# First adaptive chunks as one-column TensorE products between the first projections

## What is computed

```python
cond = jax.nn.silu(c)                                   # c: (1, 1024)
for i in range(DEPTH):                                  # 2 layers
    shift, scale, gate = jnp.split(cond @ ada_w[i] + ada_b[i], 3, axis=-1)   # ada_w[i]: (1024, 3072)
    h = rms_norm(x, norm_g[i]) * (1 + scale[:, None, :]) + shift[:, None, :]
    y = nsa_mixer(h, ...) if i % N_MIXERS == 0 else moba_mixer(h, ...)
    x = x + gate[:, None, :] * y
# in nsa_mixer
q, kc, vc, ks, vs, kw, vw, gl, z = split_cols(h @ w_in, [...])
# kc, vc go through a block compressor (gelu(flat @ cmp_w1 + b1) @ cmp_w2); ks, kw are normed and rotated
```

## Time and profile before

| | us |
|---|---|
| median of 3 runs | 1037.69 (1036.21 to 1040.94) |
| profiled execution, its own time | 1035.83 |
| its span, first to last instruction | 1034.0 |
| TensorE busy | 937.6 |
| VectorE busy | 604.4 |
| ScalarE busy | 522.7 |
| GpSimd busy | 189.5 |

### The profile page before, as it was taken

How to read it: one execution, slowest core, us unless ns; L and a number is a source line. 1 busy time by engine, 2 the same in 40 slices (tenths; PEclk the granted TensorE clock), 3 DMA queues, 4 the chain that set the end, 5 groups by cost and what they waited for, 6 DMA issues and landing times.

```text
span 1034.0 us, 13297 instructions
## 1 busy us (share of the span) xinstructions
PE 937.6 (91%) x4855; PEld 765.9 (74%) x4855; DVE 604.4 (58%) x1178; ACT 522.7 (51%) x956; POOL 189.5 (18%) x204
## 2 busy tenths in 40 slices
PE   0299998798989978989999998999899889999997
PEld 0288987455668955778888887888788778888886
DVE  5765447976457478555555544658345745555542
ACT  4243446775435477454444443667555444444431
POOL 4305504663002660000000000326000200000000
PEclk9999999987699999999999999999999999999999
DMA  8654735544055452435655653545233544555551
GB/s 314 239 188 140 235 126 172 163 147 139 0 163 166 141 183 82 156 108 176 207 168 183 203 169 113 194 143 167 81 101 111 169 146 165 183 191 196 187 160 41
DMA packets 45391, 163.28 MB, mean 158 GB/s; under 512 B 5136, under 2 KB 5392, under 8 KB 45328
## 3 DMA queue, kind: packets, MB, share of 16 engines
q1 hardware_dynamic: 45328, 162.44, 48.8%
HBM read 161.37 MB, written 1.05 MB: 157 GB/s over the span
## 4 chain that ended last, share of the span: by engine, by line
PE 80%; DVE 9%; issue 5%; ACT 4%; DMA 1%; POOL 1%; SPq 0%; POOLq 0%; DVEq 0%; ACTq 0%
PE bank L445 52%; PE bank L454 11%; PE bank L469 4%; PE bank L498 3%; PE bank L594 3%; PE bank L573 2%; PE bank L572 1%; DVE ada_acc L1367 1%; PE bank L531 1%; PE bank L596 1%; DVE soft L1460 1%; DVE stats L1449 1%; ACT soft L974 1%; PE bank L593 1%; DMA pos<-in_positions 1%
## 5 line engine op out<-in xcount | busy, mean ns | idle before, releaser
L855 ACT ACTIVATE w_hi<-w_raw 128x1024 fp32r<-128x1024 f32 (+2 forms) x249 | 259.5, 1047 | 210.7 <-PE bank L445 187.7
L1277 DVE TENSOR_TENSOR w_lo<-w_raw,w_hi 128x1024 fp32r<-128x1024 f32 (+2 forms) x249 | 300.8, 1224 | 111.0 <-ACT w_hi L855 110.9
L445 PE MATMUL bank<-w_hi,h_hi 128*128 128x512 f32 (+1 forms) x576 | 227.5, 395 | 2.7 <-DVE h_lo L1814 2.7
L445 PE MATMUL bank<-w_hi,h_lo 128*128 128x512 f32 (+1 forms) x576 | 224.2, 389 | 0.0
L445 PE MATMUL bank<-w_lo,h_hi 128*128 128x512 f32 (+1 forms) x576 | 223.8, 389 | 0.0
L445 PEld LDWEIGHTS bank<-w_hi,h_hi 128*128 128x128 f32 x576 | 108.6, 189 | 23.7 <-issue 3.0
L445 PEld LDWEIGHTS bank<-w_hi,h_lo 128*128 128x128 f32 x576 | 108.5, 188 | 22.5
L445 PEld LDWEIGHTS bank<-w_lo,h_hi 128*128 128x128 f32 x576 | 108.8, 189 | 20.8
L1895 POOL TENSOR_TENSOR ada_acc<-ada_acc,w_raw 128x512 f32<-128x512 f32 x70 | 93.1, 1330 | 87.4 <-ACT w_raw L859 80.7
L454 PE MATMUL bank<-h_hi,w_hi 128*128 128x256 f32 x264 | 77.9, 295 | 0.2 <-ACT tok_k L859 0.2
L454 PE MATMUL bank<-h_lo,w_hi 128*128 128x256 f32 x264 | 75.3, 285 | 0.0
(11 more groups left out here) (256 smaller groups left out, 1455.7 us busy)
## 6 DMA issues: line engine op xcount, KB each, us to landing
w_raw<-in_weights SPq DMA_DIRECT2D x298, 512.0 KB, 4.0
w_raw<-in_weights SPq DMA_DIRECT2D x4, 360.0 KB, 3.2
x<-in_x SPq DMA_DIRECT2D x1, 1024.0 KB, 10.2
gate_bias<-in_gate_bias SPq DMA_DIRECT2D x2, 512.0 KB, 9.1
out<-x SPq DMA_DIRECT2D x1, 1024.0 KB, 4.0
w_raw<-in_weights SPq DMA_DIRECT2D x3, 256.0 KB, 2.6
const<-in_constants SPq DMA_DIRECT2D x1, 413.5 KB, 3.1
cols<-in_columns SPq DMA_DIRECT2D x1, 208.5 KB, 3.9
```

The costliest lines, as they stand in the source:

```text
L445: mm = e.matmul(pb[t][:, 0:n], xs[q], ws[p], start=(k + kk == 0 and i == 0), stop=(k + kk == kts - 1 and i == 2))
L855: e.activation(w_hi[i % NSPLIT][:, 0:c], raw[v % NRAW][:, 0:c], ACT.Copy).then_inc(*rounded(v))
L1277: e.tensor_tensor(w_lo[i % NSPLIT][:, 0:c], raw[v % NRAW][:, 0:c], w_hi[i % NSPLIT][:, 0:c].bitcast(F32), ALU.subtract).then_inc(*rested(v))
```

## The change

- `ada_products` on TensorE takes over the first four chunks: the raw unit is the stationary operand, block by block, and `cond` the one moving column. The four results of a chunk stand in four columns of a bank, summed over the eight blocks there. ScalarE, GpSimd and VectorE no longer touch these units.
- The units are reordered: chunk 0 (shift) and chunk 2 (scale) of the first four feature blocks come first; then units of chunks 1 and 3 stand between the first two units of `nsa_kcvc` and of `nsa_kskw`, which need only those four blocks of h. TensorE's list follows that order. The pairing stands behind the third `nsa_kskw` unit, not the second.
- `norm_modulates` and `norm_rounds` run in two halves, two pairs each; a fourth bank (7) takes the fourth turned pair in the first layer.
- `rotation_tables` is split: the angles stay first on VectorE, the tables move behind the second half of `norm_modulates`. On ScalarE the squares of x stand ahead of sine and cosine.
- The first DMAs are columns, unit 0, x, constants, unit 1, positions, rows, then the other units.

```diff
-    order = (ada(0, 0, 4)
-             + one("nsa_kcvc") + one("nsa_kskw") + one("nsa_q0") + one("cmp_w1_0", CJ, 256, False)
+    early, kcvc, kskw = ada(0, 1, 2) + ada(0, 3, 4), one("nsa_kcvc"), one("nsa_kskw")
+    order = (ada(0, 0, 1) + ada(0, 2, 3)
+             + [kcvc[0]] + early[0:3] + [kcvc[1]] + early[3:6] + [kskw[0]] + early[6:8] + [kskw[1]]
+             + kcvc[2:] + kskw[2:] + one("nsa_q0") + one("cmp_w1_0", CJ, 256, False)
...
+            def ada_products(c, bank, free):
+
+                w.wait_ge(*cond_done.at())
+                w.wait_ge(*free)
+                for u in of[f"ada0_{c}"]:
+                    w.wait_ge(*fetched[u % NRAW].at(u))
+                    for kk in range(units[u][2]):
+                        k = units[u][1] + kk
+                        for j in range(4):
+                            mm = e.matmul(bank[:, j:j + 1], raw[u % NRAW][:, kk * 512 + j * P:kk * 512 + (j + 1) * P],
+                                          cond[:, k:k + 1], start=(k == 0 and j == 0), stop=(k == KT - 1 and j == 3),
+                                          skip_group_check=True)
+                    mm.then_inc(*ada_used(u))
+                    yield u
...
-            for c in range(4):
-                ada_columns(c, banks[2 * (c % 2)], ada_cols.at(c - 2) if c > 1 else const_in.at())
-            norm_turns(0, [const_in.at()] * 3)
-            whole(linear("nsa_kcvc", 0, (h_hi, h_lo), h_of(0), True, [ada_cols.at(2)]))
...
+            whole(ada_products(0, banks[0], const_in.at()))
+            norm_turns(0, [const_in.at()] * 4)
+            whole(ada_products(2, banks[2], const_in.at()))
+            kcvc = linear("nsa_kcvc", 0, (h_hi, h_lo), h_of(0), True, [ada_cols.at(0)])
+            kskw = linear("nsa_kskw", 1, (h_hi, h_lo), h_of(0), True, [ada_cols.at(2)])
+            ada1 = ada_products(1, banks[4], modulated.at((0, 0)))
+            ada3 = ada_products(3, banks[5], modulated.at((0, 1)))
+            steps_of(kcvc, 1)
+            steps_of(ada1, 3)
+            steps_of(kcvc, 1)
+            steps_of(ada1, 1)
+            steps_of(ada3, 2)
+            steps_of(kskw, 1)
+            steps_of(ada3, 2)
+            steps_of(kskw, 1)
+            whole(kcvc)
+            steps_of(kskw, 1)
...
+            rounds(of["nsa_kcvc"][0])
+            norm_rounds(0, (0, 1))
+            rounds(of["nsa_kcvc"][1])
+            rounds(of["nsa_kskw"][0])
+            rounds(of["nsa_kskw"][1], 0)
+            norm_rounds(0, (2, 3))
...
+            rotation_angles()
+            norm_factors(0, *(squared.at((0, t, j)) for t in range(TT) for j in range(2)))
+            ada_column(0, banks[0])
+            ada_column(2, banks[2])
+            rests(of["nsa_kcvc"][0])
+            norm_modulates(0, (0, 1))
+            rests(of["nsa_kcvc"][1])
+            ada_column(1, banks[4])
+            rests(of["nsa_kskw"][0])
+            ada_column(3, banks[5])
+            rests(of["nsa_kskw"][1], 0)
+            norm_modulates(0, (2, 3))
             rotation_tables()
...
-            for j in range(4):
-                sum_chunk(0, j)
             norm(0)
-            for j in range(4):
-                sum_chunk(2, j)
...
-            e.dma_start(const[:, :], const_d).then_inc(*const_in())
             e.dma_start(cols[:, :], cols_d).then_inc(*cols_in())
             fetch(0)
+            e.dma_start(x[:, :, :], x_d.rearrange("o (t p) d -> p (o t) d", p=P)).then_inc(*x_in())
+            e.dma_start(const[:, :], const_d).then_inc(*const_in())
             fetch(1)
```

More of the change, by code:

```diff
@@ L597, in attention, with steps_of @@
                                  skip_group_check=True).then_inc(*valued((s, j)))
-            for c in range(4):
-                ada_columns(c, banks[2 * (c % 2)], ada_cols.at(c - 2) if c > 1 else const_in.at())
-            norm_turns(0, [const_in.at()] * 3)
-            whole(linear("nsa_kcvc", 0, (h_hi, h_lo), h_of(0), True, [ada_cols.at(2)]))
-            for j in linear("nsa_kskw", 1, (h_hi, h_lo), h_of(0), True, [ada_done.at(0)]):
-                if j == 1:
-                    for i in range(2):
-                        w.wait_ge(*parity_even.at(1))
-                        w.wait_ge(*parity_odd.at(1))
-                        w.wait_ge(*modulated.at((0, 1 + i)))
-                        for g in range(NKV):
-                            for tt in range(TT):
-                                mm = e.matmul(banks[5 + i][:, g * P + tt * 64:g * P + (tt + 1) * 64],
-                                              by_parity[:, tt, i * NKV + g, :, :].rearrange("p l d -> p (l d)"),
-                                              con("pair"), start=True, stop=True)
-                        mm.then_inc(*tokens_paired(i))
+            def steps_of(steps, n):
+                for _ in range(n):
+                    next(steps)
@@ new lines, in tensor @@
+            steps_of(ada1, 3)
[7 more added lines that the diff above has]
+            steps_of(kskw, 1)
+            for i in range(2):
+                w.wait_ge(*parity_even.at(1))
+                w.wait_ge(*parity_odd.at(1))
+                w.wait_ge(*ada_done.at((0, 1)))
+                w.wait_ge(*modulated.at((0, 1 + i)))
+                for g in range(NKV):
+                    for tt in range(TT):
+                        mm = e.matmul(banks[5 + i][:, g * P + tt * 64:g * P + (tt + 1) * 64],
+                                      by_parity[:, tt, i * NKV + g, :, :].rearrange("p l d -> p (l d)"),
+                                      con("pair"), start=True, stop=True)
+                mm.then_inc(*tokens_paired(i))
@@ L843, in scalar, with rounds @@
             ahead = [0]
-            def rounds(u):
-                while ahead[0] <= min(u + NSPLIT - 1, len(units) - 1):
+            def rounds(u, more=NSPLIT - 1):
+                while ahead[0] <= min(u + more, len(units) - 1):
                     v = ahead[0]
@@ L867, in square_half, with norm_rounds @@
                              accum_out=halves[i][:, j * TT + t:j * TT + t + 1]).then_inc(*squared((i, t, j)))
-            def norm_rounds(i, scale=None):
-                for kp in range(KT // 2):
+            def norm_rounds(i, kps=range(KT // 2), scale=None):
+                for kp in kps:
                     k = 2 * kp
@@ L987, in scalar @@
             e.activation(cond[:, :], col("c"), ACT.Silu).then_inc(*cond_done())
-            for j in range(4):
-                scale_chunk(0, j)
+            for t in range(TT):
+                for j in range(2):
+                    square_half(0, t, j, x_in.at())
             w.wait_ge(*turns_reduced.at())
@@ L1267, in vector, with rests @@
             ahead = [0]
-            def rests(u):
-                while ahead[0] <= min(u + NSPLIT - 2, len(units) - 1):
+            def rests(u, more=NSPLIT - 2):
+                while ahead[0] <= min(u + more, len(units) - 1):
                     v = ahead[0]
@@ L1308, in rest @@
                                     ALU.subtract).then_inc(*h_rested((i, 2 * kp), (i, 2 * kp + 1)))
-                for kp in range(KT // 2):
+                for kp in kps:
+                    w.wait_ge(*ada_done.at((i, kp // 2)))
                     w.wait_ge(*x_turned.at((i, kp)))
@@ L1534, in vector @@
                 rests(u)
-                if j == 2:
+                if j == 3:
                     for i in range(2):
```

89 lines of the change are left out of this document (29 added, 60 removed).

## The result

The changed kernel takes 1064.86 us (median of 4 runs, 1063.76 to 1071.35) against 1038.79 us (4 runs, 1036.21 to 1040.94) before: 1.029 times the time, interval 1.023 to 1.035. It is 26 us slower. The profiled execution, at 1071.35 us with a span of 1069.5, was the longest of the four.

A forecast was written before the change was run, and what follows sets the result against it. TensorE, busy 91% of the span, was taken as the bound: stream start plus stream. The head's steps summed to 109.8 us against 93.30, 16.5 later, which on the median of 1037.69 gave 1054 us, range 1045 to 1064.

The forecast's parts named there:

- the milestone: Start of the compressor's products on TensorE: 93.30 us before, forecast at 109.8, 16.5 later.
- (a): First products, chunk 0: unit 1 lands at 12, three units at low clock take 10.3, end at 22.3 us.
- (b): Turns of x behind chunk 0: 5.95 us as before, to 28.3; the angles, without their brake, some 3.5.
- (c): Chunk 2's products behind the turns: 7.2 to 13.7 us, taken as 9.5, to 37.8.
- (d): Handover before the projections, TensorE waiting for VectorE's columns, split, modulation and h_lo: 4.4 us, to 42.2.
- (e): Four projection and eight product units interleaved: 25.3 to 47.8 us, taken as 36, plus 1.8 of wait, to 80.0.
- (f): Wait before the third `nsa_kcvc` unit for VectorE's modulation, tables and next w_lo: 2.6 to 5.0, taken as 3.5 us.
- (g): Three projection units 8.2, pairings 3.5, another unit 2.7 and 1.0 for low clock: to 98.9 us.
- (h): `nsa_q0`, last stretch before the compressor's products: 10.9 us, to 109.8.
- Rival A: Clock stays full through the products: compressor's products at 91.8, 1.5 us earlier, 1036 us; chance 0.22.
- Rival B: Full clock and cheap one-column records, below about 0.10 us each: 6.3 us earlier, 1031 us; chance 0.08.
- Rival D: Clock low from first product to the interleaved part's end: compressor's products about 126, 1071 us; chance 0.08.

The follow-up runs named there:

- e8: The changed kernel with the first product waiting for the landed columns of constants, not the last block of constants: 1057.16 us, ratio 1.018.
- e2: The changed kernel with the rotation tables moved ahead of the columns on VectorE, right behind the norm factors: 1056.81 us, ratio 1.025.
- e0: The kernel before, run again unaltered: 1040.0 us (10 runs, 1029.2 to 1051.1), ratio 0.9996.
- e1: The changed kernel with 128 equal moving columns in place of one in each product: 1039.31 us, ratio 1.003 to the kernel before.

## Why the prediction was wrong in size and right in kind

The sign, the milestone's mechanism and the low clock were right. The difference was 26.1 us and not 16.5: of the missing 9.6 us, 1.9 are in the sum up to the milestone and 7.7 behind it. By the steps:

- (a) Chunk 0 done at 22.3: it was 23.43. Units 0 and 1 landed in time (e8 shows 4.84 and 11.55, 12 was taken), and 0.21 us a record held (13.78 for 64). The step overlooked the wait on the constants, which now land behind x: 9.65 instead of 6.5. e8 prices it at 1.5.
- (b) Turns 5.95, measured 5.40. The angles lost their brake as said, 3.2 us for 3.5.
- (c) 9.5 for chunk 2, measured 8.88: it ends at 37.72, forecast 37.8. Full at first, low at the end, as written.
- (d) Handover 4.4, measured 4.19.
- (e) The interleaved part with its wait of 1.8: 37.8 forecast, to 80.0. Measured, from 41.91 to the end of the second `nsa_kskw` unit (5.0 us of matmuls from 77.15): 82.2, some 40 us. The wait was 1.67. The middle taken between 25.3 and 47.8 was 2.6 too low.
- (f) 3.5 of wait, measured 2.25, for the reason given; e2 removed it.
- (g), (h) From the third `nsa_kcvc` unit to the milestone 26.3 (15.4 and 10.9), measured 27.26: the low clock lasted 1 us longer.
- Sum: 109.8 forecast, 111.70 measured. 16.5 was 18.4. The closeness is luck in part: (a), (e), (g) and (h) were 4.6 us too low together, (b), (c), (d) and (f) 2.6 too high.

**The step that failed** is the sentence behind the sum: "Behind it the two kernels have the same work in the same order", from which the 16.5 of the milestone was put on the median as it stood. That is a term of nothing for the rest. Measured, the rest was 953.2 us against 945.5, 7.7 more, and 949.8 in the repetition; with the low stretches of the clock the rest of the kernel before alone moves from 942.5 to 949.5 between sets of runs. The forecast's range of 1045 to 1064 had room for the head alone: e between 28 and 44, c, and DMA. With those 7 us on top its upper end would have been 1071. The working had named the condition ("if the attention's stretch at 0.50 changes its length, which I leave as it is") and gave it no price. Its three runs of before, 5 us apart, were all it could see; e0's ten are 22 apart. Whether any of the 7.7 us belongs to the change stays open.

**Rival A** (full clock through the products, 1036) is what e1 made of the kernel with 128 columns: forecast milestone 91.8, measured 94.68. Most of the 2.9 us lies behind the wait for the tables, where 25.3 was taken and 27.26 measured, since the clock is low there in e1 as well. So its sum was nearly right and its condition wrong for one column. The Trainium skill (TensorE: Matmul & The Clock Gate, section Loop structure matters more than you think) has the clock stay up in matmuls without waits between them. The trace contradicts it for one column: 2.00 of 2.00 us busy and granted 0.50. **Rival B** fell with it: even e1's groups at the full level took 0.112 a record. **Rival D** (low throughout, milestone 126) did not come: from the group of chunk 2 on every group begins at full clock. The price for a load in the Trainium skill (same page, section LDWEIGHTS), 107 ns for 128 columns without a word on the clock, is close to the 0.112 us a record at full level and misses the low one, 20 against 11 records in 2 us.

## What to carry over

Before work is moved to the engine that bounds the kernel, take the record's price at both clock levels and ask which level the new stream keeps; here the eight product units between the projections took 14.3 us with 128 equal columns and 18.6 with one, and left the projections slower too. Move only the part for which the bounding engine is idle ahead of its stream (here chunks 0 and 2) and leave the other to the idle engine: by the ratios that was 6 to 18 us faster than before with 128 equal columns and 9 with one. The whole on TensorE was 19 to 30 us slower with one column and no faster than before with 128. Predict a milestone and check it in one profile, and price the scatter of the rest from repeated runs of the same kernel before giving a range.

## What was not expected of the hardware

- In the head the granted column prints 1.00 while records run at the low level's pace: 11 records in 15 to 17 us in the kernel after, 20 in the same window in e1. The column alone does not tell the pace; the count of records does.
- The first group took 8.92 us with 128 equal columns, 13.89 with 64 and 13.78 with one; in the later groups 64 columns did as well as 128 (5.3 and 5.36 us for 48) and 1 did not (6.93, 7.84). Which number of columns ran at which pace differed between the first group and the later ones.
- One kernel's executions range over 22 us, 1029 to 1051, at mean granted clocks from 0.972 to 0.942, and one of its low stretches comes and goes: 29 or 54 records in 430 to 440 us in two profiles of the change. Others come back to the microsecond: in every 10 us from the milestone to the end of the first attention the two profiles of before show the same granted clock to 0.01, and so do the two of the change.
- VectorE's small steps took 0.19 to 0.22 us each with GpSimd's sums gone, where every other one had taken 1.14 to 1.26.
